# Making the gates' second one-hot matrix, with the shares in it, on GpSimd, one token per instruction

## The reference, cut to what matters

```python
st, it = lax.top_k(s, PEER_TOPK)
cand = st[:, :, 0, :, None] + st[:, :, 1, None, :]
cidx = it[:, :, 0, :, None] * N_KEYS + it[:, :, 1, None, :]
best, pos = lax.top_k(cand, PEER_TOPK)
e = jnp.take_along_axis(cidx, pos, axis=-1)
g = jax.nn.softmax(best, axis=-1)
act = gelu(einsum("thkd,td->thk", take(eu, e), t))
return einsum("thk,thkd->td", g * act, take(ev, e))
```

## Time and profile before

| | |
|---|---|
| runs | 3705.19, 3707.51, 3710.32 us; median 3707.51 |
| span of the profiled execution | 3707.94 us (the page prints 3707.9) |
| PE busy | 3622.5 us, 98% of the span |
| PEld busy | 3268.6 us, 88% |
| DVE busy | 2587.6 us, 70% |
| ACT busy | 1721.3 us, 46% |
| POOL busy | 756.6 us, 20% |
| TensorE's granted clock | 0.989 |

### The profile page before, as it was taken

One profiled execution on the slowest core, in us unless ns is written; L12 is line 12 of the kernel. 1 busy time (PEld: TensorE's weight loads), 2 busy tenths in 40 slices (PEclk: granted clock), 3 DMA queues, 4 the chain that ended last, 5 costly groups with the idle time before them and its releaser, 6 DMA issues. The chain is left out here.

```text
span 3707.9 us, 66781 instructions
## 1 busy us (share of the span) xinstructions
PE 3622.5 (98%) x24114; PEld 3268.6 (88%) x24114; DVE 2587.6 (70%) x4881; ACT 1721.3 (46%) x3076; POOL 756.6 (20%) x302
## 2 busy tenths in 40 slices
PE   9999999999899999999999999999999999999998
PEld 8788899976799999888899999888777999998887
DVE  7552757587469888556578898556586698995555
ACT  4344345443345444555455444555443554444554
POOL 5555046000078000000086000000000680000000
PEclk9999999999899999999999999999999999999999
DMA  7767855421255444555555444555432454445554
GB/s 268 235 217 263 277 171 184 142 86 52 78 173 176 148 147 144 192 191 185 188 174 171 147 145 154 193 185 193 158 98 68 160 176 147 148 146 190 192 193 142
DMA packets 175143, 621.09 MB, mean 168 GB/s; under 512 B 19376, under 2 KB 25136, under 8 KB 174896
## 3 DMA queue, kind: packets, MB, share of 16 engines
q1 hardware_dynamic: 172192, 615.35, 49.7%
q10 hardware_dynamic: 2704, 2.38, 0.2%
HBM read 614.51 MB, written 1.05 MB: 166 GB/s over the span
## 5 line engine op out<-in xcount | busy, mean ns | idle before, releaser
L2441 ACT ACTIVATE ring_hi<-ring 128x1024 fp32r<-128x1024 f32 x786 | 832.4, 1059 | 507.0 <-PE bank L2370 503.2
L2313 PE MATMUL bank<-H_r,ring_hi 128*128 128x256 f32 x3232 | 932.0, 288 | 8.7 <-POOL ring_r L2298 6.5
L2315 PE MATMUL bank<-H_r,ring_r 128*128 128x256 f32 x3232 | 914.0, 283 | 0.0
L2314 PE MATMUL bank<-H_r,ring_hi 128*128 128x256 f32 x3232 | 913.8, 283 | 0.0
L290 POOL TENSOR_TENSOR ring_r<-ring,ring_hi 128x1024 fp32r<-128x1024 f32 x131 | 317.0, 2421 | 1643.7 <-ACT ring_hi L284 1643.7
L2313 PEld LDWEIGHTS bank<-H_r,ring_hi 128*128 128x128 f32 x3232 | 619.0, 192 | 11.4 <-ACT arena L2446 4.4
L2314 PEld LDWEIGHTS bank<-H_r,ring_hi 128*128 128x128 f32 x3232 | 619.7, 192 | 0.0
L2315 PEld LDWEIGHTS bank<-H_r,ring_r 128*128 128x128 f32 x3232 | 618.8, 191 | 0.0
L2298 POOL TENSOR_TENSOR ring_r<-ring,ring_hi 128x1024 fp32r<-128x1024 f32 x156 | 432.2, 2801 | 554.1 <-ACT ring_hi L2441 554.1
L2366 PE MATMUL bank<-ring_hi,w_high 128*128 128x512 f32 x1536 | 476.6, 391 | 1.8 <-DVE ring_r L2684 1.8
L2684 DVE TENSOR_TENSOR ring_r<-ring,ring_hi 128x1024 fp32r<-128x1024 f32 x390 | 474.6, 1218 | 2.5 <-ACT ring_hi L2441 2.5
(11 more groups left out here) (446 smaller groups left out, 5833.9 us busy)
## 6 DMA issues: line engine op xcount, KB each, us to landing
ring<-in_peer_u SPq DMA_DIRECT2D x384, 512.0 KB, 3.2
ring<-in_peer_v SPq DMA_DIRECT2D x384, 512.0 KB, 3.3
ring<-in_w_in SPq DMA_DIRECT2D x135, 512.0 KB, 3.6
arena<-in_ada SPq DMA_DIRECT2D x96, 512.0 KB, 5.6
ring<-in_w_f SPq DMA_DIRECT2D x72, 512.0 KB, 3.5
ring<-in_w_br SPq DMA_DIRECT2D x24, 512.0 KB, 4.7
ring<-in_w_out SPq DMA_DIRECT2D x24, 512.0 KB, 3.2
ring<-in_w_q SPq DMA_DIRECT2D x24, 512.0 KB, 3.3
```

The costliest lines, as they stand in the source:

```text
L2313: pe.matmul(o, hi[:, k], x_hi_[:, kt, :], start=(kt == 0), stop=False)
L2314: pe.matmul(o, hi[:, k], x_lo_[:, kt, :], start=False, stop=False)
L2315: mm = pe.matmul(o, lo[:, k], x_hi_[:, kt, :], start=False, stop=(kt == KT - 1))
L2441: act.activation(ring_hi[:, m % NH, :], ring[:, (n0 + m) % NS, :], ACT.Copy).then_inc(a_hi, 1)
```

## The change

The multiplied one-hot matrix is made on POOL. For every token one `tensor_scalar` of 128x128 compares `iota` with the token's column number and multiplies with its share, both taken as scalars for each partition (`cols_[:, t:t + 1]` and `wts[:, t:t + 1]`). Four of them make a quad; the last counts the new semaphore `p_col`. POOL waits once for `a_t`, then from the third quad on for `g_ps`. PE's `build` waits for `p_col` besides `v_hot`. On DVE `hit_keys` and `weigh_keys` become one `hit_rows` with the comparison for `hotA` alone, which stands where `hit_keys` stood; the comparison for `hotB`, its multiplication and the wait for `v_col` between them go.

```diff
@@ gpsimd
+                        def weighted_keys(q):
+                            if q >= 2:
+                                pool.wait_ge(g_ps, q - 1)
+                            for u in range(4):
+                                t = 4 * q + u
+                                ins = pool.tensor_scalar(hotB[:, q % 2, u, :], cc("iota"), cols_[:, t:t + 1], wts[:, t:t + 1],
+                                                         ALU.is_equal, ALU.mult)
+                            ins.then_inc(p_col, 1)
+
+                        pool.wait_ge(a_t, TT)
+                        for q in range(QUADS):
+                            weighted_keys(q)
@@ tensor
                         def build(q):
                             pe.wait_ge(v_hot, q + 1)
+                            pe.wait_ge(p_col, q + 1)
                             if q >= 4:
                                 pe.wait_ge(a_rest, q - 3)
@@ vector
-                        def hit_keys(q):
+                        def hit_rows(q):
                             if q >= 2:
                                 dve.wait_ge(g_ps, q - 1)
                             r = slice(4 * q, 4 * q + 4)
-                            dve.tensor_tensor(hotB[:, q % 2, :, :], cc("iota").unsqueeze(1).to_broadcast([P, 4, P]),
-                                              cols_[:, r].unsqueeze(2).to_broadcast([P, 4, P]), ALU.is_equal).then_inc(v_col, 1)
-
-                        def weigh_keys(q):
-                            r = slice(4 * q, 4 * q + 4)
                             dve.tensor_tensor(hotA[:, q % 2, :, :], cc("iota").unsqueeze(1).to_broadcast([P, 4, P]),
-                                              rows_[:, r].unsqueeze(2).to_broadcast([P, 4, P]), ALU.is_equal)
-                            dve.wait_ge(v_col, q + 1)
-                            dve.tensor_tensor(hotB[:, q % 2, :, :], hotB[:, q % 2, :, :],
-                                              wts[:, r].unsqueeze(2).to_broadcast([P, 4, P]), ALU.mult).then_inc(v_hot, 1)
+                                              rows_[:, r].unsqueeze(2).to_broadcast([P, 4, P]), ALU.is_equal).then_inc(v_hot, 1)
...
                         for q in range(2):
-                            hit_keys(q)
-                            weigh_keys(q)
+                            hit_rows(q)
                         for c in range(C0, NK):
                             quads = quads_at(c)
                             for q in quads:
                                 gate(q)
                                 if q + 2 < QUADS:
-                                    hit_keys(q + 2)
+                                    hit_rows(q + 2)
                             if c + 3 < NK:
                                 low_up(c + 3)
-                            for q in quads:
-                                if q + 2 < QUADS:
-                                    weigh_keys(q + 2)
                             if c > G0:
                                 gate_late(c - 1)
```

More of the change, by code:

```diff
@@ L2277, in build @@
                 with Phase("keys_in", "by_q", "s_ps", "a_s", "v_read", "v_diff", "a_e", "v_found", "t_ps", "a_t",
-                           "v_chain", "a_hi", "p_lo", "a_gelu", "v_col", "v_hot", "a_hot", "g_ps", "v_g", "a_rest", "v_late", "v_ulo", "v_lo", "a_whi",
+                           "v_chain", "a_hi", "p_lo", "a_gelu", "p_col", "v_hot", "a_hot", "g_ps", "v_g", "a_rest", "v_late", "v_ulo", "v_lo", "a_whi",
                            "v_w", "e_sq", "e_sum", "e_root", "e_norm", "e_high", "e_chain", "n_normed", "n_high", "n_low") as (
                         block, keys_in, by_q, s_ps, a_s, v_read, v_diff, a_e, v_found, t_ps, a_t,
-                        v_chain, a_hi, p_lo, a_gelu, v_col, v_hot, a_hot, g_ps, v_g, a_rest, v_late, v_ulo, v_lo, a_whi, v_w,
+                        v_chain, a_hi, p_lo, a_gelu, p_col, v_hot, a_hot, g_ps, v_g, a_rest, v_late, v_ulo, v_lo, a_whi, v_w,
                         e_sq, e_sum, e_root, e_norm, e_high, e_chain, n_normed, n_high, n_low):
```

## The result

The changed kernel takes 3773.45 us (median of four runs, 3773.26 to 3774.61) against 3708.91 for the kernel before (four runs, 3705.19 to 3713.74): slower by 64.5 us, a ratio of 1.0172 with a 95% interval of 1.0157 to 1.0186. The profiled execution has a span of 3771.6 us against 3707.9.

The account below looks back on a forecast made before the run. PE was taken to bound the gate stages; 3707.94 us of the profiled execution + 0 + 0 + 0, less 0.43 for the median of runs, gave 3707.5, said as 3708 us, range 3701 to 3768.

Parts of the forecast that it names:

- What bounds the kernel now: In the three gate stages PE sets the time, busy for all 281.00 us of each, with DVE 88% busy.
- The gain: Taking 230 us of work from DVE in the gate stages saves 0 us, covered by PE's own queue of matmuls.
- What is added on POOL: Four 128x128 instructions a quad in the gate stages, 0.40 us each (0.20 to 0.90), 1.6 us of a quad's 4.39.
- What POOL and DVE do to each other: In the gate stages POOL's instructions hold DVE's two-SBUF-input ones; DVE then needs 4.28 or 3.88 us a quad, cost 0 us.
- 4 x p: POOL's own time a quad in the gate stages: four instructions at 0.40 us each, 1.6 us.
- The first rival: In rows with a quad DVE becomes the bound because POOL holds it: about +60 us, 3768 us, chance 0.27.
- ahead of L2352 with POOL as the releaser: Sign that the forecast is wrong: PE idle ahead of source line L2352, released by POOL.
- The new wait on PE: PE's added wait for p_col ahead of each build, 192 of them: 0 to 1.9 us, taken as 0.
- The first build: Each gate stage's first build: in time at 0.40 us an instruction; 1.8 us late at 0.90, 5.5 us in three stages.
- DVE's work: L2640 and L2648 go from the gate stages, 1.20 us a quad, 230 us of DVE's work in all.

Follow-up runs that it names:

- the quarters: The changed kernel with each DVE subtraction of 128x1024 from row 48 on made as four of 128x256: 3721.3 us, ratio 1.0027 to the kernel before.
- the fifth instruction: The changed kernel with a fifth POOL instruction of the same form in each quad, into a tile that nobody reads: 3910.5 us in one run.
- short subtraction: The changed kernel with DVE's subtraction from row 48 on cut from 1024 to 64 columns, the rest left out: 3712.2 us in one run.
- multiplication on POOL: The kernel before with POOL doing only the multiplication by the shares, one 128x512 tensor_tensor a quad, DVE comparing for both matrices: 3713.5 us, ratio 0.9997.

## Why the prediction was wrong

- **What bounds the kernel now** held: in each of the seven runs in which the matrix was made in time (all but the quarters, the fifth instruction and the changed kernel), the build stretch is 274.7 to 274.9 us, with DVE busy for 100.4 us of the 281 from the first build on (short subtraction) or for 261.5 (multiplication on POOL). The gain of 0 held as well.
- **What is added on POOL** failed in its size. I took 0.40 us, by the subtraction's 2.35 ns a column and 0.10 fixed; it is 0.78 us, by 3.3 ns a column and 0.37 fixed, the pointer reads included. My range of 0.20 to 0.90 holds it, but the value that the sum used is half of it. The row that I called nearest reads no scalar and was long, so its fixed part could not be seen in it.
- **What POOL and DVE do to each other** is the step that failed, and it decided the case. From the earlier trace rows I read that the engines take turns, and then counted the turns on one side: how long POOL holds DVE. The same rows say what DVE does to POOL (8.71 us for two subtractions that take 4.80 alone), and I never added that to POOL's 4 x p. The four instructions have 3.13 us of their own and 1.57 us of waiting, 4.70 against 4.39. At the full price of 0.78 us but with shorter waits the stage holds, as the run with the short subtraction shows (a mean of 0.880, 3.52 a quad). So the waits were needed for the loss. Whether the price was needed too is open: with the same waits and my 0.40 it would be 1.6 + 1.57 = 3.17, which fits, but this is an estimate and no run has such an instruction in the kernel, and by itself the one of 8 columns (0.401 alone) waited longer than the one of 128 (1.820 and 1.912 in all). In the other direction my count was far too high: I took up to 0.40 us of holding of DVE for each POOL instruction, 1.20 or 1.60 a quad; measured were at most some 0.12 a quad.
- I wrote that POOL "is far from the bound even if it waits". For the first build of a stage I did count waits of POOL, three of them, 2.34 of the 3.94 us, and did not carry them over to the other 63 quads.
- A reading in the same part was too wide. I wrote that DVE instructions with one tensor in SBUF keep their time beside POOL, next to a copy with one input in SBUF that was held for 2.27 us. For the gate, on which the count rests, it held: the median of L2657, now L2663, is 0.522 us before and after.
- The section "Who interferes with whom" of the Trainium skill's "SBUF — State Buffer" says that the one that starts second waits. These runs agree that both can be the one that waits (POOL for 1.57 us a quad here, DVE's subtraction for 0.84 us beside the multiplication on POOL); but the small POOL instructions, 0.8 us long, left the median of DVE's additions at 0.679 and lengthened the distance of their starts by 0.03 us in the mean, so they didn't shut DVE out for their whole length.
- **The first rival** (chance 0.27) had the amount, +60 us, by luck and for the wrong reason: DVE became lighter and idle, and POOL the bound. That POOL becomes the bound stood in no rival of mine. I had its sign at what would be seen, "ahead of L2352 with POOL as the releaser".
- **The new wait on PE**: 0, as forecast. **The first build**: I said in time at 0.40 and 1.8 us late at 0.90. It was 2.27 us late at 0.78, 6.8 us of the 64. POOL's four began at 1195.43 and took 6.1 us, 3.1 of their own and 3.0 of waiting; I had allowed 2.34 for two comparisons and one subtraction, and in that time DVE ran two of each.
- **DVE's work**: it fell by 207 us, not by the full 230. The comparison left on DVE took 9.0 us more in sum and the subtraction 3.2; of the rest I can't say how much is held time, since an instruction that follows an idle stretch no longer overlaps its neighbour.

## What to carry to other kernels

When two engines take turns at reading SBUF, add the waits to both. Take the engine that gets the new work first: its price alone, plus, for every scalar that it takes through a pointer, the length of what the other engine has running. Many small GpSimd instructions with such scalars beside long two-input VectorE instructions were the worst mix of those tried; one wide instruction without pointers (a mean of 1.421 us for a shortest of 1.352, ratio 0.9997 here) or shorter pieces on VectorE cost far less. And a stage that one engine fills without a gap gains nothing when another engine is relieved; such a move can only lose.

## What the runs showed of the hardware that was not expected

- A `tensor_scalar` of 128x128 on GpSimd takes 0.79 us alone with two pointer scalars, 0.60 with one and a comparison only, 0.64 with two numbers. A `tensor_tensor` product of the same size takes 0.45.
- Beside VectorE additions with two SBUF inputs, started every 0.60 us, each pointer scalar adds some 0.60 us: 0.72, 1.32, 1.91 us. Eight columns with two pointers cost 1.82.
- The holding is lopsided. The small instructions with two pointers lengthen a VectorE instruction little (means of 1239 ns for 1226 and 731 for 683), while one GpSimd `tensor_tensor` of 128x512 of 1.42 us lengthens the subtraction from 1.22 to 2.06.
- The same instruction on VectorE is listed with 0.34 us, four of them with as much as two of 128x512; but four overlap at their ends, 1.11 us of busy time a quad, and beat the two passes by ten microseconds a stage.
